# A buffer of its own for the second gate, the gates' results moved in memory, and two steps reordered in a hybrid attention and expert layer

## The chip, the cores and the metric

The kernel runs on one NeuronCore of one Trainium2 chip. The metric is the device time of one execution in microseconds (us). Five engines work side by side, each on its own list of instructions in order: TensorE (PE; its weight loads are listed as PEld), VectorE (DVE), ScalarE (ACT), GpSimd (POOL) and SyncE (SP), which here issues nearly all DMA transfers. They meet at semaphores only.

## What is computed

One encoder layer on 1024 tokens of width 1024, in float32. Cut to what matters here:

```python
# token mixing: branch A is gated linear attention, two directions per head, 4 heads
la_f = log_sigmoid(gaf @ gla_wa2_f + gla_ba_f) / 16      # first gate (forward)
la_b = log_sigmoid(gab @ gla_wa2_b + gla_ba_b) / 16      # second gate (backward)
o_a  = gla(q, k, v, la_f) + flip(gla(flip(q), flip(k), flip(v), flip(la_b)))
y_a  = (rmsnorm(o_a) * silu(gr)) @ w_gla_out
# branch B is a multi-head latent attention, y_b = o_b @ w_mla_out
g = sigmoid(gates)
x = x + (g[..., :D] * y_a + g[..., D:] * y_b) @ w_o      # the merge
# channel mixing: 16 experts, each takes the 128 tokens that suit it best
for e in range(16):
    rows = h[idx[e]]
    out[idx[e]] += vals[e] * ((silu(rows @ w_gate[e]) * (rows @ w_up[e])) @ w_down[e])
```

## The kernel before

Every large product is done as three matmuls (`three`, L825): each operand is split into a high part, rounded for TensorE's fast float32 mode, and a low part, what the rounding left. For weights ScalarE writes the high part (`dense_hi`, L1967; `split` of the experts, L2174) and VectorE subtracts it for the low part (`dense_lo`, L1381; `split`, L1800; both record their instruction at L1264). TensorE waits for the low part. The order of the work on each engine is written out by hand.

Three stretches matter.

**The heads of the gated attention** (`gla_head`, four of them: L992 on TensorE, L1537 on VectorE, L2031 on ScalarE). For each of two gates (d = 0, 1) TensorE makes the logits (L954), VectorE adds the bias into `zT` (`gate_bias`, L1541), ScalarE forms `eT` in three passes (L2053 to L2057), VectorE scans it into `bT` (L1563), subtracts half a chunk's value (L1570), and writes the tail, the distance to the end of the chunk, over `zT` (L1576). ScalarE then makes the exponentials `qt`, `kt` from `bT` and `kd` from `zT` (L2064 to L2067), copies the head's projected queries and keys (`take_qk`, L2034) and goes on to the second gate. VectorE's bias for d = 1 waits for that `kd` (`ed_ok`, L1544), because it overwrites `zT`. Meanwhile TensorE runs `project_vr` (L964): tiles 6 and 7 first, then 4 and 5, which need the banks of the second gate's logits and so wait for its bias (`z_dve`, L971), then 0 to 3, which wait for the copies of queries and keys (L973).

**The merge** (`job`, L1058): jobs in the order of `ORDER` (L59), four gates first, then outputs and gates in turn, 48 matmuls each. ScalarE takes a gate's logits through a sigmoid into `sg` (`gate`, L2098), two slots in turn. Gate job 2 writes the banks of gate 0, so it waits for that sigmoid (L1066). `sg` lies at the start of `merge_mem`, over `oaS`, the last head's output on its way to DRAM, so ScalarE waits at L2095 until this is stored (`oa_out`). The outputs come back as `mT` (L646, L650) and are split into `oT_hi` and `oT_lo` (`branch_hi` L2112, `branch_lo` L1679). SyncE stores the last head's output (L648), waits for it (L649), loads it again, and only then loads the weights of gate job 3 and on (L651).

**The start of the experts.** 24 units of 128 x 1024 weights per expert, in a ring of 8 slots for the split parts and 24 raw slots. VectorE splits units 0 to 15 (L1846), multiplies the first expert's gate and up products (`activate(0)`, L1848), and in `turn(0)` splits units 16 and on, with the low parts of the second expert's rows (`rows_in`, L1804) ahead of units 20 and 24. TensorE needs those halves before the units 16 and 20 (`gate`, L1208) and transposes `act_r` behind unit 20.

Of the kernel before, what the change touches and what calls it, by code (L numbers as in the profile page):

```python
# [8 lines left out]
P = 128  # L9
# [4 lines left out]
ALU = mybir.AluOpType  # L14
# [4 lines left out]
S = 1024  # L19
# [134 lines left out]
def hybrid_layer(nc, x, positions, g_mix, w_in, gla_wa2_f, gla_ba_f, gla_wa2_b, gla_ba_b, gla_onorm,  # L154
# [25 lines left out]
    with ExitStack() as ctx:  # L180
# [29 lines left out]
        with mix_mem:  # L210
# [69 lines left out]
            with late_mem:  # L280
# [10 lines left out]
                with gla_tmp:  # L291

                    out_mem = ExitStack()
                    with out_mem:
                        oaS = sb_in(out_mem, "oaS", [P, 2, S])
                    vr = sb_in(gla_tmp, "vr", [P, NT, 2 * DV])
                    qk_T = sb_in(gla_tmp, "qk_T", [P, 2, S])
                    qt = sb_in(gla_tmp, "qt", [P, 2, S])
                    kt = sb_in(gla_tmp, "kt", [P, 2, S])
                    kd = sb_in(gla_tmp, "kd", [P, 2, S])  # L300
                    zT = sb_in(gla_tmp, "zT", [P, S])
                    eT = sb_in(gla_tmp, "eT", [P, S])
                    bT = sb_in(gla_tmp, "bT", [P, S])
                    near = sb_in(gla_tmp, "near", [P, 2, NSC])
                    decay = sb_in(gla_tmp, "decay", [P, 2, NSC])
                    keep_hi = sb_in(gla_tmp, "keep_hi", [P, 2, P])
                    keep_lo = sb_in(gla_tmp, "keep_lo", [P, 2, P])
                    scan_m = sb_in(gla_tmp, "scan_m", [P, S])
                    kdR = qk_T[:, :, :].rearrange("p d (t c) -> p d t c", t=NT)
                    oR = kd[:, :, :].rearrange("p a (t c) -> p (a t) c", c=DV)  # L310
                    o_sqr = kt[:, :, :].rearrange("p a (t c) -> p (a t) c", c=DV)
                    att = bT[:, :].rearrange("p (t c) -> p t c", t=NT)
                    att_f = zT[:, :].rearrange("p (t c) -> p t c", t=NT)
                    att_b = eT[:, :].rearrange("p (t c) -> p t c", t=NT)
                merge_mem = ExitStack()
                with merge_mem:
                    sg = sb_in(merge_mem, "sg", [P, 2, S])
                    branch_mem = ExitStack()
# [938 lines left out]
        def _(dve):  # L1257
# [279 lines left out]
            def gla_head(h, first=False, more=True):  # L1537
# [3 lines left out]
                def gate_bias(d):  # L1541
                    dve.wait_ge(z_mm, h * 2 + d + 1)
                    if d == 1:
                        dve.wait_ge(ed_ok, h * 2 + 1)  # L1544
                    dve.tensor_scalar(zT[:].rearrange("p (a c) -> p a c", a=2), ps[:, 6 - 2 * d:8 - 2 * d, :],  # L1545
                                      b_a2[:, d:d + 1], None, ALU.add).then_inc(z_dve, 1)

                for d in range(2):
                    if d == 0:
                        gate_bias(0)  # L1550
                        if not first:
# [3 lines left out]
                    dve.wait_ge(z_act, h * 6 + 3 * d + 3)  # L1555
                    dve.scalar_tensor_tensor(out=eT[:], in0=zT[:], scalar=0.0, in1=eT[:], op0=ALU.min,
                                             op1=ALU.subtract).then_inc(ls_ok, 1)
# [16 lines left out]
                    if d == 1:  # L1574
                        dense_lo(4, mine)
                    dve.tensor_tensor(zT[:].rearrange("p (n c) -> p n c", c=P), last.broadcast_to((P, NSC, P)), b3,  # L1576
                                      ALU.subtract).then_inc(tail_ok, 1)
# [4 lines left out]
                    if d == 0:  # L1582
                        gate_bias(1)
                        dense_lo(3, mine)
                        dve.wait_ge(qk_ev, h * 4 + 4)
                    else:
                        dense_lo(5, mine)
# [238 lines left out]
            def turn(e, first=False, last=False):  # L1826
                for u in range(UNITS):
                    if first and u in (4, 8):
                        rows_in(1, (u // 4 - 1,))
                    split(FIRST + u, e)  # L1830
# [15 lines left out]
            for n in range(4, FIRST):  # L1846
                split(n)
            activate(0)  # L1848
            turn(0, first=True)
# [10 lines left out]
        def _(act):  # L1860
# [170 lines left out]
            def gla_head(h, first=False, last=False):  # L2031
# [17 lines left out]
                for d in range(2):  # L2049
                    act.wait_ge(z_dve, h * 2 + d + 1)  # L2050
                    if d == 1:
                        act.wait_ge(b_ok, h * 2 + 1)
                    nc.scalar.activation(eT[:], zT[:], ACT.Abs).then_inc(z_act, 1)  # L2053
                    act.wait_ge(z_act, h * 6 + 3 * d + 1)
# [11 lines left out]
                    act.wait_ge(tail_ok, h * 2 + d + 1)  # L2066
                    nc.scalar.activation(kd[:, d, :], zT[:], ACT.Exp, scale=1 / GATE_DIV).then_inc(ed_ok, 1)  # L2067
                    if d == 0:
# [25 lines left out]
            second_half_T(GH - 1, bank=4)  # L2094
            act.wait_ge(oa_out, 16 * GH)  # L2095

# [15 lines left out]
            def branch_hi(b, rows=range(KD)):  # L2112
                for k in rows:
                    if b:
                        act.wait_ge(stage_in[k % 2], 16 * (k // 2) + 16)
                    else:
                        act.wait_ge(oa_back, 16 if k < 6 else 32)
                    src = stage[:, k % 2, :] if b else mT[:, k, :]
                    nc.scalar.activation(oT_hi[:, k, :], src, ACT.Copy).then_inc(oT_hi_ok, 1)
# [86 lines left out]
            def turn(e, first=False, last=False):  # L2206
                for u in range(UNITS):
                    if first and u in (4, 8):
                        rows_in(1, (u // 4 - 1,))
                    split(FIRST + u, e)  # L2210
# [52 lines left out]
```

## Time and profile before

| | |
|---|---|
| time, median of 3 runs | 2054.45 us (2053.08 to 2058.4) |
| the profiled execution: its time, its span | 2054.51 us, 2052.8 us |
| mean granted TensorE clock | 0.981 of full |
| TensorE busy | 1939.7 us (94%) |
| VectorE busy | 1268.2 us (62%) |
| ScalarE busy | 981.9 us (48%) |
| GpSimd busy | 119.4 us (6%) |
| chain that ended last | TensorE 87%, VectorE 8%, ScalarE 2% |
| DMA, mean over the span | 148 GB/s, but 380 to 400 in the expert stretch |

The span runs from the first to the last instruction; the time has 1.7 us around it. Latent attention takes the time to about 590 us, the four heads to 970, the merge and the output projection to 1430, the choice of tokens to 1480, and the experts the rest. In the timeline's rows the columns are start, duration (both us), engine, line, operation, output<-input, shapes and count; in brackets stands the engine's idle time before it and what ended that.

### The profile page before, as it was taken

Reading aid. Unit: us, or ns where it says so; the run is one execution under the profiler, and the core shown is the slowest. Engines: PE = TensorE matmul, PEld = TensorE weight load, DVE = VectorE, ACT = ScalarE, POOL = GpSimd, SP = SyncE. Lnnn points to the kernel's source line nnn. Section 1 sums busy time; section 2 is a strip of 40 time slices with the busy share of each in tenths; the row PEclk is TensorE's granted clock in tenths of the full one; section 3 lists DMA queues with packets and bytes.
Section 4 is the critical chain, followed back from the end, with each engine's and each line's share of the span. In section 5 each row is a group of like instructions: output and inputs, shape, how many; then the busy total and the mean of one; then the engine's idle time right before and its main releaser. Section 6 shows DMA issues by size and latency. Waiting matters only on the chain.

```text
span 2052.8 us, 25988 instructions
## 1 busy us (share of the span) xinstructions
PE 1939.7 (94%) x9268; PEld 1605.5 (78%) x9268; DVE 1268.2 (62%) x1660; ACT 981.9 (48%) x1588; POOL 119.4 (6%) x127
## 2 busy tenths in 40 slices
PE   7989999999999999999899999999289999999997
PEld 5677888888778787878688888887278888888886
DVE  4157777777865646565311222432978989898986
ACT  4155555555454334242311211322268787878785
POOL 2010000000000000000000000000001010101010
PEclk9999999999999999999999999999699999999999
DMA  6000000000311111120412311152789999999992
GB/s 238 0 17 12 21 18 22 22 22 6 107 53 43 53 42 52 31 62 9 156 52 65 110 52 52 62 208 90 282 312 380 400 394 399 395 398 397 397 398 80
DMA packets 138658, 303.11 MB, mean 148 GB/s; under 512 B 16208, under 2 KB 70864, under 8 KB 138576
## 3 DMA queue, kind: packets, MB, share of 16 engines
q1 hardware_dynamic: 133968, 285.20, 37.3%
q0 software_dynamic: 4608, 16.78, 3.2%
q8 instruction: 55, 0.90, 0.2%
q14 instruction: 27, 0.22, 0.0%
HBM read 272.58 MB, written 29.36 MB: 147 GB/s over the span
## 4 chain that ended last, share of the span: by engine, by line
PE 87%; DVE 8%; ACT 2%; issue 1%; DMA 1%; POOL 1%; SPq 0%; DVEq 0%; ACTq 0%; POOLq 0%
PE ps L827 21%; PE ps L829 21%; PE ps L828 21%; PE ps L780 6%; PE ps L851 5%; PE ps L808 2%; PE ps L809 2%; PE ps L1042 1%; PE ps L885 1%; PE ps L884 1%; PE ps L1054 1%; DVE row_max L1445 1%; PE ps L1148 1%; PE ps L1026 1%; DVE top_i L1780 1%
## 5 line engine op out<-in xcount | busy, mean ns | idle before, releaser
L1264 DVE TENSOR_TENSOR w_lo<-w_raw,w_hi 128x1024 fp32r<-128x1024 f32 x384 | 442.7, 1218 | 57.8 <-ACT w_hi L2180 57.6
L2180 ACT ACTIVATE w_hi<-w_raw 128x1024 fp32r<-128x1024 f32 x384 | 370.9, 1052 | 12.6 <-PE ps L829 8.0
L1264 DVE TENSOR_TENSOR d_lo<-d_raw,d_hi 128x1024 fp32r<-128x1024 f32 x58 | 71.0, 1224 | 311.9 <-ACT d_hi L1972 311.8
L1972 ACT ACTIVATE d_hi<-d_raw 128x1024 fp32r<-128x1024 f32 x58 | 61.5, 1061 | 308.9 <-PE ps L829 296.9
L827 PE MATMUL ps<-w_hi,xeT_hi 128*128 128x512 f32 x512 | 201.8, 394 | 7.1 <-DVE xeT_lo L1264 7.1
L829 PE MATMUL ps<-w_hi,xeT_lo 128*128 128x512 f32 x512 | 200.1, 391 | 0.0
L828 PE MATMUL ps<-w_lo,xeT_hi 128*128 128x512 f32 x512 | 200.0, 391 | 0.0
L827 PE MATMUL ps<-hT_parts,d_hi 128*128 128x512 f32 x384 | 152.2, 396 | 8.5 <-ACT sg L2105 7.7
L828 PE MATMUL ps<-hT_parts,d_hi 128*128 128x512 f32 x384 | 150.6, 392 | 0.0
L829 PE MATMUL ps<-hT_parts,d_lo 128*128 128x512 f32 x384 | 150.6, 392 | 0.0
L1445 DVE TENSOR_REDUCE row_max<-ps 128x1 f32<-128x1024 f32 x64 | 78.3, 1224 | 106.6 <-PE ps L885 105.9
L723 POOL TENSOR_TENSOR stat<-stat,minus_half 128x1 f32<-128x1 f32 (+3 forms) x48 | 57.2, 1191 | 1286.0 <-DVE stat L1261 1286.0
L827 PE MATMUL ps<-d_hi,hT_parts 128*128 128x512 f32 x288 | 113.8, 395 | 6.9 <-DVE zT L1545 6.9
L827 PEld LDWEIGHTS ps<-w_hi,xeT_hi 128*128 128x128 f32 x512 | 96.7, 189 | 27.1 <-issue 6.3
L828 PE MATMUL ps<-d_lo,hT_parts 128*128 128x512 f32 x288 | 112.8, 392 | 0.0
L829 PE MATMUL ps<-d_hi,hT_parts 128*128 128x512 f32 x288 | 112.7, 391 | 0.0
L829 PEld LDWEIGHTS ps<-w_hi,xeT_lo 128*128 128x128 f32 x512 | 96.5, 189 | 20.3
L828 PEld LDWEIGHTS ps<-w_lo,xeT_hi 128*128 128x128 f32 x512 | 96.7, 189 | 19.5
L827 PE MATMUL ps<-w_hi,act_T_hi 128*128 128x512 f32 x256 | 101.0, 395 | 0.8 <-ACT ye L2203 0.8
L828 PE MATMUL ps<-w_lo,act_T_hi 128*128 128x512 f32 x256 | 99.7, 389 | 0.0
L829 PE MATMUL ps<-w_hi,act_T_lo 128*128 128x512 f32 x256 | 99.7, 389 | 0.0
L827 PE MATMUL ps<-oT_hi,d_hi 128*128 128x512 f32 x256 | 99.6, 389 | 0.0
(313 smaller groups left out, 4006.7 us busy)
## 6 DMA issues: line engine op xcount, KB each, us to landing
w_raw<-in_w_gate_e SPq DMA_DIRECT2D x128, 512.0 KB, 8.0
w_raw<-in_w_up_e SPq DMA_DIRECT2D x128, 512.0 KB, 7.5
w_raw<-in_w_down_e SPq DMA_DIRECT2D x128, 512.0 KB, 6.7
d_raw<-in_w_in SPq DMA_DIRECT2D x80, 256.0 KB, 3.0
xs<-in_x SPq DMA_DIRECT2D x8, 512.0 KB, 6.9
rows_T<-hT SPq DMA_DIRECT2D x1, 4096.0 KB, 12.8
mla_out_T<-obS SPq DMA_DIRECT2D x16, 256.0 KB, 2.0
carry<-rows_T SPq DMA_DIRECT2D x1, 4096.0 KB, 14.2
```

The source lines that it names most:

```text
L723: pool.tensor_tensor(dst, dst, minus_half[:, 0:dst.shape[1]], ALU.pow).then_inc(done, 1)
L780: ins = pe.transpose(ps[0:rows, bank, j * P:(j + 1) * P], src, ident[:])
L808: pe.matmul(ps[:, a, 0:LA], lhs, w_lat[:, k, 0:LA], start=k == 0, stop=k == KD - 1)
L809: mm = pe.matmul(ps[:, b, 0:LB], lhs, w_lat[:, k, LA:LAT], start=k == 0, stop=k == KD - 1)
L827: pe.matmul(out_ap, a_hi, b_hi, start=start, stop=False)
L828: pe.matmul(out_ap, a_hi, b_lo, start=False, stop=False)
L829: return pe.matmul(out_ap, a_lo, b_hi, start=False, stop=stop)
L851: mm = pe.matmul(ps[:, bank, j * width:(j + 1) * width], src[:, k, t * P:(t + 1) * P], w[:, k, :], start=k == 0, stop=k == kc - 1)
L1264: return dve.tensor_tensor(dst, whole, high.bitcast(F32), ALU.subtract)
L1445: dve.tensor_reduce(row_max[:, n:n + 1], ps[:, 2 * (n % 2):2 * (n % 2) + 2, :], mybir.AxisListType.XY, ALU.max, negate=True).then_inc(max_ ...
L1972: nc.scalar.activation(d_hi[:, n % 2, :], d_raw[:, n % 2, :], ACT.Copy).then_inc(d_hi_ok, 1)
L2180: nc.scalar.activation(w_hi[:, n % RING, :], w_raw[:, n % RAW, :], ACT.Copy).then_inc(hi_ok, 1)
```

## The change

Four edits, none of which adds or removes arithmetic.

- The second gate's biased logits go to a buffer of their own, `zT_back`; the wait for `ed_ok` is gone, and VectorE adds that bias ahead of the first gate's tail instead of behind the decay.
- `sg` moves behind the place of `oT_hi` and `oT_lo` (16 x S + HALF elements further on), and so no longer lies over `oaS`. ScalarE's wait for the store stands now in front of the copies into `oT_hi`, behind the first two gates' sigmoids.
- VectorE takes the low parts of the second expert's rows ahead of units 16 and 18 instead of 20 and 24, and `activate(0)` ahead of unit 19 instead of ahead of 16.
- ScalarE takes the second half of those rows ahead of unit 22 instead of 24.

```diff
--- before.py
+++ after.py
@@ -299,6 +299,7 @@
                     kt = sb_in(gla_tmp, "kt", [P, 2, S])
                     kd = sb_in(gla_tmp, "kd", [P, 2, S])
                     zT = sb_in(gla_tmp, "zT", [P, S])
+                    zT_back = sb_in(gla_tmp, "zT_back", [P, S])
                     eT = sb_in(gla_tmp, "eT", [P, S])
                     bT = sb_in(gla_tmp, "bT", [P, S])
                     near = sb_in(gla_tmp, "near", [P, 2, NSC])
@@ -314,7 +315,10 @@
                     att_b = eT[:, :].rearrange("p (t c) -> p t c", t=NT)
                 merge_mem = ExitStack()
                 with merge_mem:
-                    sg = sb_in(merge_mem, "sg", [P, 2, S])
+                    sg_mem = ExitStack()
+                    with sg_mem:
+                        sb_in(sg_mem, "below_sg", [P, 16 * S + HALF])
+                        sg = sb_in(sg_mem, "sg", [P, 2, S])
                     branch_mem = ExitStack()
                     with branch_mem:
                         oT_hi = sb_in(branch_mem, "oT_hi", [P, KD, S], F32R)
@@ -1540,9 +1544,7 @@
 
                 def gate_bias(d):
                     dve.wait_ge(z_mm, h * 2 + d + 1)
-                    if d == 1:
-                        dve.wait_ge(ed_ok, h * 2 + 1)
-                    dve.tensor_scalar(zT[:].rearrange("p (a c) -> p a c", a=2), ps[:, 6 - 2 * d:8 - 2 * d, :],
+                    dve.tensor_scalar((zT, zT_back)[d][:].rearrange("p (a c) -> p a c", a=2), ps[:, 6 - 2 * d:8 - 2 * d, :],
                                       b_a2[:, d:d + 1], None, ALU.add).then_inc(z_dve, 1)
 
                 for d in range(2):
@@ -1553,7 +1555,8 @@
                         dense_lo(2, mine)
 
                     dve.wait_ge(z_act, h * 6 + 3 * d + 3)
-                    dve.scalar_tensor_tensor(out=eT[:], in0=zT[:], scalar=0.0, in1=eT[:], op0=ALU.min,
+                    z = (zT, zT_back)[d]
+                    dve.scalar_tensor_tensor(out=eT[:], in0=z[:], scalar=0.0, in1=eT[:], op0=ALU.min,
                                              op1=ALU.subtract).then_inc(ls_ok, 1)
                     dve.wait_ge(ls_ok, h * 2 + d + 1)
 
@@ -1573,14 +1576,15 @@
                     last = b3[:, :, 0:1] if d else b3[:, :, P - 1:P]
                     if d == 1:
                         dense_lo(4, mine)
-                    dve.tensor_tensor(zT[:].rearrange("p (n c) -> p n c", c=P), last.broadcast_to((P, NSC, P)), b3,
+                    else:
+                        gate_bias(1)
+                    dve.tensor_tensor(z[:].rearrange("p (n c) -> p n c", c=P), last.broadcast_to((P, NSC, P)), b3,
                                       ALU.subtract).then_inc(tail_ok, 1)
                     dve.wait_ge(e_ok, h * 6 + 3 * d + 2)
                     e3 = qt[:, d, :].rearrange("p (n c) -> p n c", c=P)
                     s.link(dve.tensor_tensor(decay[:, d, :].unsqueeze(2), e3[:, :, 0:1] if d else e3[:, :, P - 1:P],
                                              near[:, d, :].unsqueeze(2), ALU.mult))
                     if d == 0:
-                        gate_bias(1)
                         dense_lo(3, mine)
                         dve.wait_ge(qk_ev, h * 4 + 4)
                     else:
@@ -1825,8 +1829,10 @@
 
             def turn(e, first=False, last=False):
                 for u in range(UNITS):
-                    if first and u in (4, 8):
-                        rows_in(1, (u // 4 - 1,))
+                    if first and u in (0, 2):
+                        rows_in(1, (u // 2,))
+                    if first and u == 3:
+                        activate(0)
                     split(FIRST + u, e)
                     if u == (8 if first else 2) + LEAD - 1:
                         act_in(e, 0)
@@ -1845,7 +1851,6 @@
             rows_in(0)
             for n in range(4, FIRST):
                 split(n)
-            activate(0)
             turn(0, first=True)
             with dve.Fori(1, NE - 2) as e:
                 turn(e)
@@ -2050,7 +2055,7 @@
                     act.wait_ge(z_dve, h * 2 + d + 1)
                     if d == 1:
                         act.wait_ge(b_ok, h * 2 + 1)
-                    nc.scalar.activation(eT[:], zT[:], ACT.Abs).then_inc(z_act, 1)
+                    nc.scalar.activation(eT[:], (zT, zT_back)[d][:], ACT.Abs).then_inc(z_act, 1)
                     act.wait_ge(z_act, h * 6 + 3 * d + 1)
                     nc.scalar.activation(eT[:], eT[:], ACT.Exp, scale=-1.0).then_inc(z_act, 1)
                     act.wait_ge(z_act, h * 6 + 3 * d + 2)
@@ -2064,7 +2069,7 @@
                     nc.scalar.activation(qt[:, d, :], bT[:], ACT.Exp, scale=1 / GATE_DIV).then_inc(e_ok, 1)
                     nc.scalar.activation(kt[:, d, :], bT[:], ACT.Exp, scale=-1 / GATE_DIV).then_inc(e_ok, 1)
                     act.wait_ge(tail_ok, h * 2 + d + 1)
-                    nc.scalar.activation(kd[:, d, :], zT[:], ACT.Exp, scale=1 / GATE_DIV).then_inc(ed_ok, 1)
+                    nc.scalar.activation(kd[:, d, :], (zT, zT_back)[d][:], ACT.Exp, scale=1 / GATE_DIV).then_inc(ed_ok, 1)
                     if d == 0:
                         take_qk()
                         dense_hi(3, mine)
@@ -2092,7 +2097,6 @@
                 gla_head(h)
             gla_head(GH - 1, last=True)
             second_half_T(GH - 1, bank=4)
-            act.wait_ge(oa_out, 16 * GH)
 
 
             def gate(b, i):
@@ -2114,6 +2118,7 @@
                     if b:
                         act.wait_ge(stage_in[k % 2], 16 * (k // 2) + 16)
                     else:
+                        act.wait_ge(oa_out, 16 * GH)
                         act.wait_ge(oa_back, 16 if k < 6 else 32)
                     src = stage[:, k % 2, :] if b else mT[:, k, :]
                     nc.scalar.activation(oT_hi[:, k, :], src, ACT.Copy).then_inc(oT_hi_ok, 1)
@@ -2205,8 +2210,8 @@
 
             def turn(e, first=False, last=False):
                 for u in range(UNITS):
-                    if first and u in (4, 8):
-                        rows_in(1, (u // 4 - 1,))
+                    if first and u in (4, 6):
+                        rows_in(1, (u // 2 - 2,))
                     split(FIRST + u, e)
                     if u == LEAD - 1 and not first:
                         results(e - 1)
```

## Rows read from the trace of the kernel before

**Rows 1.** TensorE's waits: who waited for whom, us in total, times, longest.

```profile
PE ps L827 <- ACT sg L2105: 7.7, 1, 7.7
PE ps L827 <- DVE xeT_lo L1264: 7.1, 2, 6.1
PE ps L827 <- DVE zT L1545: 6.9, 4, 2.1
```

**Rows 2.** Timeline of TensorE, merge, matmuls at full clock.

```profile
1014.53 0.39 PE L828 MATMUL ps<-hT_parts,d_hi 128*128 128x512 f32 x1
...
1015.66 0.39 PE L827 MATMUL ps<-oT_hi,d_hi 128*128 128x512 f32 x1
```

**Rows 3.** Timelines of VectorE, ScalarE and TensorE, second head.

```profile
703.06 1.23 DVE L1576 TENSOR_TENSOR zT<-bT 128x1024 f32<-128x1024 f32 x1
...
706.22 1.28 DVE L1545 TENSOR_SCALAR zT<-ps,b_a 128x1024 f32<-128x1024 f32 x1 [1.79 <-ACT kd L2067]
...
706.02 2.04 ACT L2038 ACTIVATE qk_T<-ps 128x512 f32<-128x512 f32 x4
...
707.56 0.50 PE L827 MATMUL ps<-d_hi,hT_parts 128*128 128x512 f32 x1 [2.01 <-DVE zT L1545]
```

**Rows 4.** Timeline of TensorE, third and fourth head, at tile 4.

```profile
800.81 0.50 PE L827 MATMUL ps<-d_hi,hT_parts 128*128 128x512 f32 x1 [1.98 <-DVE zT L1545]
...
893.83 0.50 PE L827 MATMUL ps<-d_hi,hT_parts 128*128 128x512 f32 x1 [2.08 <-DVE zT L1545]
```

**Rows 5.** Busy time by stretch, fourth head: length, engines (instructions), PEclk, DMA share, GB/s.

```profile
894.00:898.00 4.00, 4.00 (x11) 3.15 (x12) 2.72 (x3) 3.94 (x5) 0.00 (x0) 0.57 0.12 16
```

**Rows 6.** Timelines of TensorE, ScalarE and VectorE, start of the merge.

```profile
982.96 0.39 PE L829 MATMUL ps<-hT_parts,d_lo 128*128 128x512 f32 x1
...
987.49 1.06 ACT L1972 ACTIVATE d_hi<-d_raw 128x1024 fp32r<-128x1024 f32 x1 [8.73 <-DMA gla_out_T<-oaS]
...
989.86 1.02 ACT L2105 ACTIVATE sg<-ps 128x1024 f32<-128x1024 f32 x1
994.14 1.06 ACT L1972 ACTIVATE d_hi<-d_raw 128x1024 fp32r<-128x1024 f32 x1 [3.26 <-DMA d_raw<-in_w_in]
...
995.23 1.23 DVE L1264 TENSOR_TENSOR d_lo<-d_raw,d_hi 128x1024 fp32r<-128x1024 f32 x1 [5.42 <-ACT d_hi L1972]
997.10 9.18 DVE L1264 TENSOR_TENSOR oT_lo<-carry,oT_hi 128x1024 fp32r<-128x1024 f32 x8 [0.64 <-ACT oT_hi L2119]
```

**Rows 7.** Chain of work that ended last, start of the merge: start, us, what.

```profile
973.15 5.62 DMA d_raw<-in_w_in
```

**Rows 8.** Timelines of VectorE, ScalarE and TensorE, start of the experts.

```profile
1495.48 5.76 DVE L1264 TENSOR_TENSOR w_lo<-w_raw,w_hi 128x1024 fp32r<-128x1024 f32 x5 [4.50 <-ACT w_hi L2180]
1504.91 1.23 DVE L1814 TENSOR_TENSOR act_r<-ps,silu_g 128x1024 f32<-128x1024 f32 x1 [3.67 <-PE ps L829]
...
1510.60 0.68 DVE L1264 TENSOR_TENSOR xeT_lo<-ps,xeT_hi 128x512 fp32r<-128x512 f32 x1
...
1502.93 0.58 ACT L2187 ACTIVATE xeT_hi<-ps 128x512 fp32r<-128x512 f32 x1
1503.41 3.89 ACT L2180 ACTIVATE w_hi<-w_raw 128x1024 fp32r<-128x1024 f32 x4
...
1511.38 0.77 PE L827 MATMUL ps<-w_hi,xeT_hi 128*128 128x512 f32 x1 [6.13 <-DVE xeT_lo L1264]
...
1525.36 0.39 PE L827 MATMUL ps<-w_hi,xeT_hi 128*128 128x512 f32 x1
```

**Rows 9.** Busy time by stretch, a stretch of expert turns; columns as in rows 5.

```profile
1606.00:1639.00 33.00, 33.00 (x152) 27.43 (x151) 29.59 (x30) 26.78 (x30) 3.62 (x2) 1.00 1.03 396
```

**Rows 10.** The raw weights' tile: duration ns min/median/max, first and last start us.

```profile
L2180 ACT ACTIVATE w_hi<-w_raw x384: 1039/1052/1065, 1437.5 to 2035.1; 128x1024 fp32r<-128x1024 f32 x192
...
L687 SPq DMA_DIRECT2D w_raw<-in_w_down_e x128: 327/333/333, 1488.9 to 2004.9; - x128
```

**Rows 11.** DMA issues of the page: count, KB each, us to landing.

```profile
w_raw<-in_w_gate_e SPq DMA_DIRECT2D x128, 512.0 KB, 8.0
```

## The prediction

> **What bounds the kernel now.** TensorE does. The table of the page gives it 94% of the span and lets nearly the whole chain of work that ended last run over it, so a change can win only where TensorE stands still. I therefore read the list of TensorE's waits first. It is led by waits that the diff does not touch (the top-k search, the start); below them stand the three of [rows 1], 7.7, 7.1 and 6.9 us in total. Each belongs to a place that the diff edits. Then I read, engine by engine, the timeline around the three. Two numbers serve throughout. A matmul of 512 columns starts every 0.226 us at full clock (five slots between 1014.53 and 1015.66 [rows 2]). A record of such a matmul lasts 0.39 us, so a wait shown as idle costs 0.39 - 0.23 = 0.16 us more in starts than the idle says.
>
> **Part A, the second gate's buffer.** In each head of the gated attention, TensorE does tiles 6 and 7 of the value product and then waits at tile 4 for the bias of the second gate's logits (L971). That bias step (L1545) writes zT, which ScalarE still reads for kd of the first gate, so VectorE waits for kd. In the second head VectorE idles 1.79 us, starts the bias at 706.22, and TensorE goes on at 707.56 after 2.01 us idle [rows 3]. With zT_back the step needs only z_mm and VectorE's own place, now right behind the subtraction of L1570, that is where the tail (L1576) begins today: 703.06. It takes 1.28 us and ends at 704.34, while TensorE is ready at 705.55. The wait goes entirely: 2.17 us of starts in this head, 2.14 and 2.24 in the third and fourth (1.98 and 2.08 idle [rows 4]). The list has 6.9 us for four waits [rows 1], so the first is 6.9 - 2.01 - 1.98 - 2.08 = 0.83, or 0.99 in starts. Sum 7.5 us. A first matmul after a wait takes 0.34 us of its slot instead of 0.23 (0.1 us, three heads: 0.3). In the fourth head the granted clock is 0.57 in the four microseconds behind the wait, level 1.2 GHz for most of it: 11 matmuls start in 4.00 us where 17.6 fit [rows 5], a loss of 6.6 x 0.23 = 1.5 us, with the edges 1.8. **A = 9.6 us.** I take that clock loss as caused by the wait, since nothing else stands still there; its bounds are 0 and 1.8. The Trainium skill, "TensorE: Matmul & The Clock Gate", section "What's actually happening", says that how many matmuls run slowly is run-variable. By that rule the third head's wait without a slow stretch and the fourth's with one would be chance, and A could be 7.8 as well as 9.6; the trace (one of three equal waits) agrees.
>
> What A delays: the tail moves 1.14 us back on VectorE (the bias's 1.28 less the overlap of neighbouring records) and ends at 704.20 + 1.23 = 705.43. ScalarE's kd, which today runs in the 0.95 us before 706.02, waits for it and comes 0.4 us later, and so does all that is queued behind it: the four copies of qk_T (2.04 us, first done now near 706.9), d_hi of the next unit, the second gate's Abs. TensorE wants the first copy at tile 0, twelve matmuls behind tile 4: 705.4 + 2.7 = 708.1, so there is 1.2 us to spare. VectorE's own idle time in front of d_lo L1264 takes up the bias step. Price zero; if that cover were gone it would cost at most the 0.4 us a head, 1.6.
>
> **Part B, the merge.** ScalarE waits at L2095 until the last head's output is stored, because sg lies over oaS. It stands 8.73 us until 987.49, then does d_hi, the table load and sg, ready at 989.86 + 1.02 = 990.88 [rows 6]. TensorE, out of work at 982.96 + 0.23 = 983.19, needs both d_lo and that sg for gate job 2. With sg elsewhere the wait moves to branch_hi, behind the first two gates. ScalarE is free at 978.76; the unit it needs landed at 978.77 (973.15 + 5.62 [rows 7]). The same block then runs 8.7 us earlier: sg at 982.15, d_lo near 981.1. Job 2 starts at 983.19 with no wait, and takes 48 x 0.226 = 10.9 us to 994.1.
> What is late next: gate job 3. The diff leaves SyncE's order alone, and there job 3's load is still queued behind the wait for the store (over at 987.49). Its d_hi starts at 994.14, when the load lands, its d_lo ends at 995.23 + 1.23 = 996.46 [rows 6]. So job 3 starts at 996.55, after a new wait of 2.5 us, and ends at 1007.4. Output job 0 needs oT_lo (997.10 + 9.18 = 1006.28) and the d_lo that follows it, done at 1007.4: just in time. The load for it is issued a microsecond sooner, behind job 3's, which may cost that one 0 to 0.5 us. Output job 0 starts today at 1015.66 and then at 1007.5: 8.2 us. The new 2.5 us wait is the size of those in [rows 4], one of which was followed by a slow stretch and one not, so I take half of 1.8 off: **B = 7.3 us**, bounds 8.2 and 6.0.
> ScalarE's moved wait has the eight oT_hi copies behind it, as before; by then (996) the store is long done, so it costs nothing.
>
> **Part C, the first experts.** VectorE has the lows of units 0 to 15 done at 1495.48 + 5.76 = 1501.24, then stands 3.67 us for activate(0), does four lows, and at 1510.60 the first half of the rows (0.68 us), with four more lows ahead of the second. TensorE waits 6.13 us for the first half and restarts at 1511.38 [rows 8]. In the new order the first half follows xeT_hi at 1503.51 and ends at 1504.2. A low takes 5.76 / 5 = 1.15 us (1.23 the last), so 16 and 17 end at 1505.4 and 1506.5. TensorE, free at 1505.25, starts near 1505.45. ScalarE now gives the second xeT_hi after two splits (1503.41 + 2 x 0.95 = 1505.3, done near 1505.95), VectorE the second low at 1507.1, low 18 at 1508.25, activate(0) at 1508.2 to 1509.4, low 19 at 1510.55. A unit takes TensorE 6 x 0.227 = 1.36 us, so it wants low 19 at 1509.7 and waits 0.9 us there, a small new wait; the transposes of act_r behind unit 20 find it ready. Counting on (three units to 1512.0 incl. that wait, a fourth, 0.8 us of transposes, three more), the next product starts at 1518.35 instead of 1525.36. **C = 7.0 us**, bounds 6 (clock low after 0.9 us) and 8 (no wait at 19). The loads of units 40 and on are issued about 2 us sooner, as lows 16 and on are.
>
> **Sum** against the profiled execution's own 2054.51 us (span 2052.8 and 1.7 around it; the median is 2054.45, so no correction): 9.6 + 7.3 + 7.0 = 23.9, and 2054.5 - 23.9 = 2030.6.
>
> **The rivals.**
> 1. A larger new wait in the merge. Job 3's load is a chain of store, 1 MB load and unit load that nothing shortens. If it lands 0.5 us later and TensorE runs all of its first stretch at the low level, B is 5; if A's clock loss also turns up elsewhere, 4.1 us are missing: 2034.7. For it: the DMA wait of 3.26 us at this very place [rows 6]. Against: its landing is set by transfers that the diff does not move.
> 2. C is hidden by transfers. In the expert turns the DMA queues are full: share 1.03, 396 GB/s, while TensorE is also busy 33.00 of 33 us [rows 9]. If the loads bound the turns, starting 7 us earlier would be given back: 2054.5 - 16.9 = 2037.6. Against: the last load is issued at 2004.9 and the last split starts at 2035.1 [rows 10], 30 us, of which a landing takes 8.0 [rows 11].
> 3. Slower than before. The same loads slow down once two expert turns are pushed together. A turn moves 24 units, a gather and a scatter of 0.524 MB each, 13.6 MB, in 13.6 / 0.396 = 34.4 us. 22 us of lead over 14 turns stand against this rival, so a turn of loads may grow from 34.4 to 36.0 us before TensorE feels it; from 37.7 us on it has eaten the 23.9 us too. A rate lower by a tenth makes the turn 38.2: 14 x 3.8 = 53, less 22 and 24, gives +7, or 2061. Nothing in the rows makes the rate fall so far.
> The Trainium skill, "DMA: Bandwidth & Descriptors", section "Where 436 GB/s comes from", holds that transfers from HBM are bound near 358 GB/s a core, which would be a turn of about 38 us and this rival's time. The trace disagrees, with 396 GB/s over whole turns.
> 4. The change does not do what it says: in A the bias still comes late, since it sits behind the scan. Then 2040; the 1.2 us between 704.34 and 705.55 speaks against.
>
> **How the numbers follow.** Forecast 0.76 (2028 to 2033), rival 1 0.11, rival 2 0.06, rival 3 0.02, rival 4 0.02, anything else 0.03. The low end takes all upper bounds (9.6 + 8.2 + 8 = 25.8: 2028.7) less a microsecond for the spread of runs; the high end reaches rival 2. About 0.3% (6 us) is what a measurement of this kernel tells from no change. Only cases that lose 18 us of the 24 come within it.
>
> **What would show it.** Right: no wait for zT at L827 in four heads; bias before tail on VectorE; no sg wait, but one near 994 of 2 to 3 us for d_lo, ended by a load; the wait for xeT_lo below 0.5 us and one near 1 us for w_lo; expert turns still of 34.4 us. Wrong: a wait for qk_T at tile 0, a split waiting for w_raw in later turns, slow stretches in new places.

## The result, and the profile after

| | before | after |
|---|---|---|
| time, median | 2054.33 us (2053.08 to 2058.4, 4 runs) | 2033.99 us (2033.06 to 2035.2, 4 runs) |
| the profiled execution: its time, its span | 2054.51 us, 2052.8 us | 2035.2 us, 2033.5 us |
| TensorE busy | 1939.7 us (94%) | 1934.6 us (95%) |

The ratio is 0.9898, 95% interval 0.9881 to 0.9915. The time lies 3.4 us above the forecast of 2030.6. That is 1.0 us above the 2028 to 2033 that the prediction gave for its forecast case, and inside its whole range, whose high end reaches the 2037.6 of rival 2. Between the two profiled executions lie 19.3 us, where 23.9 were forecast.

I cut the span at five instants of TensorE, read from its timeline, in every kernel alike: the first matmul of the first head's gate logits (L954); the start of the second half of gate job 1, 24 matmuls before the wait of [rows 1]; the first matmul of an output job (`oT_hi`); the first of the experts; and the first of the second expert's up product, the one at 1525.36 in [rows 8].

| stretch, us | before | after | won | forecast |
|---|---|---|---|---|
| start to the heads | 598.27 | 598.89 | -0.6 | 0 |
| heads (part A) | 379.38 | 369.24 | 10.1 | 9.6 |
| start of the merge (part B) | 38.01 | 35.21 | 2.8 | 7.3 |
| merge, output projection, choice of tokens | 466.60 | 466.31 | 0.3 | 0 |
| first expert (part C) | 43.10 | 36.19 | 6.9 | 7.0 |
| from there to the end | 527.44 | 527.66 | -0.2 | 0 |

So the whole shortfall lies in B. The list of TensorE's waits of the kernel after (who waited for whom, us in total, times, longest):

```profile
PE ps L784 <- DVE xs L1273: 13.5, 1, 13.5
PE ps L831 <- ACT sg L2109: 5.4, 1, 5.4
...
PE ps L831 <- DVE xeT_lo L1268: 1.0, 1, 1.0
PE ps L831 <- DVE w_lo L1268: 0.9, 2, 0.6
```

Against [rows 1]: the wait for zT is gone from it, xeT_lo fell from 7.1 to 1.0 us, and sg fell from 7.7 only to 5.4, where the prediction had it at zero. The wait for xs is the kernel's opening load; it differs from run to run, and with it the -0.6 of the first row.

Part A, the second head, VectorE's timeline of after:

```profile
701.75 0.69 DVE L1573 TENSOR_TENSOR bT<-bT,near 128x512 f32<-128x512 f32 x1
702.57 1.28 DVE L1547 TENSOR_SCALAR zT_back<-ps,b_a 128x1024 f32<-128x1024 f32 x1
703.77 1.22 DVE L1581 TENSOR_TENSOR zT<-bT 128x1024 f32<-128x1024 f32 x1
```

The bias stands directly behind the subtraction, where the tail stood in [rows 3], with no idle time in brackets. ScalarE's `kd` of this gate now waits 0.44 us for the tail, where the prediction had 0.4, and nothing behind it is late. From the first gate logits on, TensorE has no idle time over 0.15 us in the four heads and no slow stretch (a row of matmuls that start 0.43 us apart instead of 0.23, at the 1.2 GHz level).

Part B, the start of the merge, ScalarE, then TensorE, of after:

```profile
967.98 1.27 ACT L2033 ACTIVATE oaS<-ps,onorm_c 128x512 f32<-128x512 f32 x2 [4.82 <-PE ps L784]
975.66 1.06 ACT L1977 ACTIVATE d_hi<-d_raw 128x1024 fp32r<-128x1024 f32 x1 [6.42 <-DMA d_raw<-in_w_in]
976.74 1.28 ACT L2109 ACT_TABLE_LOAD   x1
978.03 1.02 ACT L2109 ACTIVATE sg<-ps 128x1024 f32<-128x1024 f32 x1
...
973.44 0.39 PE L833 MATMUL ps<-hT_parts,d_lo 128*128 128x512 f32 x1
979.20 0.77 PE L831 MATMUL ps<-hT_parts,d_hi 128*128 128x512 f32 x1 [5.37 <-ACT sg L2109]
979.76 0.63 PE L832 MATMUL ps<-hT_parts,d_hi 128*128 128x512 f32 x1
```

ScalarE is free at 969.2 and no longer waits for the store `gla_out_T<-oaS`, as in [rows 6], but for a load: the weights of gate job 2. That load lands at 975.6, and the same block of d_hi, table load and sg follows it unshortened. TensorE then stands 5.37 us and starts at the lower clock level: the stretch 979 to 984 (length, engines with their instructions, granted clock, DMA share, GB/s) has 11 matmuls and a granted clock of 0.50, the 1.2 GHz level.

```profile
979.00:984.00 5.00, 4.80 (x11) 3.80 (x12) 0.00 (x0) 0.05 (x1) 0.00 (x0) 0.50 0.92 308
```

Where the load comes from is in the view of SyncE's own issues (start, time for issuing, line) and in the view of DMAs for 945 to 975 us of after (count, size, median us from issue to landing):

```profile
962.62 0.37 SPq L650 DMA_DIRECT2D carry<-gla_out_T  x1
963.03 1.09 SPq L541 DMA_DIRECT2D d_raw<-in_w_in  x2
969.32 0.39 SPq L613 DMA_DIRECT2D gla_out_T<-oaS  x1
```

```profile
carry<-gla_out_T SPq DMA_DIRECT2D x1, 3072.0 KB, 11.5
gla_out_T<-oaS SPq DMA_DIRECT2D x1, 1024.0 KB, 8.8
d_raw<-in_w_in SPq DMA_DIRECT2D x2, 256.0 KB, 11.5
```

Half a megabyte of weights takes 11.5 us, as long as the 3 MB return issued 0.4 us before it. The same view of before, 955 to 985 us, has it too, and the prediction did not use it:

```profile
carry<-gla_out_T SPq DMA_DIRECT2D x1, 3072.0 KB, 11.4
gla_out_T<-oaS SPq DMA_DIRECT2D x1, 1024.0 KB, 8.6
d_raw<-in_w_in SPq DMA_DIRECT2D x2, 256.0 KB, 11.6
```

Issued at 972.56 and 973.1, the load of before landed near 985.0, only 2.5 us ahead of the store at 987.49. That is what moving sg could win while the load stays where it is. TensorE's wait fell by 7.7 - 5.4 = 2.3 us. Behind it 11 matmuls started at the low level where before there were 13, which is another 0.4 us of the 2.8.

Part C, the start of the experts, VectorE and TensorE of after:

```profile
1490.96 0.69 DVE L1268 TENSOR_TENSOR xeT_lo<-ps,xeT_hi 128x512 fp32r<-128x512 f32 x1 [2.29 <-ACT xeT_hi L2192]
...
1493.84 0.68 DVE L1268 TENSOR_TENSOR xeT_lo<-ps,xeT_hi 128x512 fp32r<-128x512 f32 x1
...
1495.57 1.22 DVE L1818 TENSOR_TENSOR act_r<-ps,silu_g 128x1024 f32<-128x1024 f32 x1
...
1492.93 0.47 PE L831 MATMUL ps<-w_hi,xeT_hi 128*128 128x512 f32 x1 [0.26 <-DVE w_lo L1268]
...
1497.98 0.50 PE L831 MATMUL ps<-w_hi,xeT_hi 128*128 128x512 f32 x1 [0.61 <-DVE w_lo L1268]
```

The 6.13 us of [rows 8] have become 0.26 and 0.61, and the next product starts 6.9 us sooner. About 2 of the 6.9 us are a slow stretch: in before, the first ten matmuls behind the 6.13 us wait take 4.4 us (1511.38 to 1515.78) instead of 2.3, and after has no such stretch here. Two of them, TensorE of before, 0.43 us apart:

```profile
1511.94 0.63 PE L828 MATMUL ps<-w_lo,xeT_hi 128*128 128x512 f32 x1
1512.37 0.63 PE L829 MATMUL ps<-w_hi,xeT_lo 128*128 128x512 f32 x1
```

A stretch of the expert turns, columns as in [rows 9]:

```profile
1594.00:1627.00 33.00, 33.00 (x155) 27.50 (x154) 29.58 (x30) 25.61 (x29) 3.61 (x2) 1.00 1.03 396
```

The turns run as before: TensorE full, 396 GB/s.

### The profile page after: what moved, and what is told of

It is laid out like the page before. It is cut to its first block, busy times and chain, and to the rows that moved or that the text cites. A ratio compares the mean times of both kernels' runs of the same rounds, so it can differ in the third digit from the quotient of the medians.

```text
span 2033.5 us, 25996 instructions
## 1 busy us (share of the span) xinstructions
PE 1934.6 (95%) x9268; PEld 1602.6 (79%) x9268; DVE 1267.1 (62%) x1660; ACT 981.8 (48%) x1588; POOL 120.1 (6%) x127
## 3 DMA queue, kind: packets, MB, share of 16 engines
q1 hardware_dynamic: 133968, 285.20, 37.5%
## 4 chain that ended last, share of the span: by engine, by line
PE 89%; DVE 6%; ACT 2%; DMA 1%; issue 1%; POOL 1%; SPq 0%; DVEq 0%; ACTq 0%; POOLq 0%
PE ps L831 22%; PE ps L833 22%; PE ps L832 22%; PE ps L784 6%; PE ps L855 5%; PE ps L812 2%; PE ps L813 2%; PE ps L1046 1%; PE ps L889 1%; PE ps L888 1%; PE ps L1058 1%; DVE row_max L1449 1%; PE ps L1152 1%; PE ps L1030 1%; DMA d_raw<-in_w_in 1%
## 5 line engine op out<-in xcount | busy, mean ns | idle before, releaser
L832 PEld LDWEIGHTS ps<-w_lo,xeT_hi 128*128 128x128 f32 x512 | 96.2, 188 | 19.3
```

The source lines that it names most:

```text
L832: pe.matmul(out_ap, a_hi, b_lo, start=False, stop=False)
```

## The experiments

Every result below is a median; the kernel before, run beside them on the same chips, had medians of 2054.65 to 2054.93 us; in brackets stand the ratio to it and its 95% interval. The kernel after was not run again beside them, so differences to it are best read from the stretches. These are the ones of the table above, each from one profiled execution. The theory they start from: A, B and C are independent, and B is short because the load of gate job 2 lands with the 3 MB ahead of it. The rivals: the parts disturb one another; B is short because of the store, of ScalarE's block, or of the 1 MB behind it.

**One part at a time.** The first kernel is before plus part A whole, the second leaves out the bias step's new place:

```diff
+                    zT_back = sb_in(gla_tmp, "zT_back", [P, S])
...
-                    if d == 1:
-                        dve.wait_ge(ed_ok, h * 2 + 1)
...
+                    else:
+                        gate_bias(1)
```

> Part A alone, on the kernel before. The two traces put it at 10.1 us (the last matmul ahead of the merge's wait starts at 973.44 instead of 982.96, and the run's heads began 0.6 us later), where the prediction had 9.6. Theory: the parts act at separate places and add up, so 2054.3 - 10.1 = 2044.2, and no slow stretch of TensorE in the fourth head. Rival: the fourth head's slow stretch was chance; then it turns up again somewhere in the heads and the gain is near 8 us, 2046.

> The second gate's buffer without the move: the bias stays behind the decay on VectorE. Theory: what held the bias back was the wait for kd, not its place; without it, it starts at once behind the decay, about 1.4 us later than in the full change, and ends some 0.2 us after TensorE is ready in heads two to four. Gain 8.5 to 9.5 us, 2045.3; TensorE waits for zT 0.2 us in three heads and not in the first. Rival: the place is what counts and the buffer alone gives less than half, above 2049.

Measured: 2043.72 us (0.9937, 0.9921 to 0.9954) and 2045.67 (0.9956, 0.9939 to 0.9973). The heads took 369.23 us with the whole of A, as in the kernel after, and 370.79 with the buffer alone. So the buffer carries 8.6 of the 10.1 us (1.6 of them the slow stretch in the fourth head), the new place of the bias 1.5. TensorE's waits of the second kernel show what is left without it:

```profile
PE ps L828 <- DVE zT_back L1544: 1.0, 3, 0.3
```

Three waits of 0.3 us; the first head has none. Neither kernel has a slow stretch in the heads.

The third kernel is before with `sg` moved and the wait in its new place (the diff's `sg_mem` and `oa_out` lines), the fourth is before with the new orders of the experts alone (the diff's two `turn` hunks):

> Part B alone. The traces put it at 2.8 us (from the last matmul ahead of the wait to output job 0: 32.7 before, 29.9 after), not 7.3. Theory: the same here, 2051.5, because the load of gate job 2 lands about 12 us after its issue and its d_hi, the table load and sg come only then; TensorE's wait is 5.4 us, and ScalarE waits for a load ahead of that d_hi. Rival: B is worth 7 us by itself and lost in the changed kernel because the heads end earlier; then 2047.

> Part C alone. The traces put it at 6.9 us from the first expert matmul to the second expert's up product (43.1 before, 36.2 after). Theory: 2054.3 - 6.9 = 2047.4, expert turns as before, and the wait for xeT_lo gone. Rival: the loads give part of it back over the turns once nothing else is changed; then 2049 or more and a later stretch of TensorE waiting for low parts.

Measured: 2052.33 us (0.9986, 0.9976 to 0.9995) and 2048.68 (0.9971, 0.996 to 0.9983). The start of the merge took 34.90 us, 3.1 less than before, the first expert 36.12, 7.0 less. Both kernels keep the heads of before, and there lost 1.6 us more than before did (380.94 and 380.98): two of the three 2.0 us waits for zT were followed by a slow stretch instead of one. ScalarE and TensorE in the third kernel:

```profile
987.49 1.06 ACT L1975 ACTIVATE d_hi<-d_raw 128x1024 fp32r<-128x1024 f32 x1 [6.39 <-DMA d_raw<-in_w_in]
...
991.02 0.77 PE L830 MATMUL ps<-hT_parts,d_hi 128*128 128x512 f32 x1 [5.33 <-ACT sg L2107]
```

The same wait for the same load, without A and C. The parts add up: 10.15 + 3.11 + 6.98 = 20.2 against 19.9 for the three together over the same stretches. The rival of parts that disturb one another falls.

**The load alone.** The kernel after with the load of gate job 2 ahead of the wait for the heads' stores and so ahead of the 3 MB, then with those of jobs 2 and 3:

```diff
-            load_jobs(0, 0, 2)
+            load_jobs(0, 0, 4)
             sp.wait_ge(oa_out, 16 * (GH - 1))
...
-            load_jobs(0, 2, 3)
             store_oa(GH - 1)
...
-            load_jobs(0, 3, JOBS)
+            load_jobs(0, 4, JOBS)
```

(shown for both jobs; for job 2 alone the bounds are 3, and the last call stays.)

> The changed kernel with one more edit: SyncE issues the load of gate job 2 ahead of the 3 MB return of the first six output tiles instead of behind it. Theory: that load was late because it shares the DMA queues with the 3 MB ahead of it. It has then long landed, ScalarE does d_hi, table load and sg right behind its copies of oaS, and TensorE's wait of 5.4 us in front of gate job 2 is gone, with the slow stretch behind it. Next late is gate job 3, with a wait of about 2.5 us. B becomes what was predicted for it: output job 0 starts 5.4 us sooner, 2034.0 - 5.4 = 2028.6. Rival: the load was not the cause (the table load and the sigmoid behind the copies of oaS are); then the wait stays and the time is 2034.

> As the run before, and the load of gate job 3 too ahead of the 3 MB return, so ahead of SyncE's wait for the store. Theory: both waits of TensorE in front of gate jobs 2 and 3 are gone, the copies into oT_hi start near 976 and wait only for the last 1 MB of the return near 983, the lows and the unit of output job 0 are ready before gate job 3 ends, so output job 0 starts about 7.8 us sooner than in the changed kernel: 2026.2. Rival: the later return of the outputs, now behind 1 MB of loads, becomes the bound, and this run is no better than the one before, 2028.6.

Measured: 2027.76 us (0.9864, 0.9848 to 0.9881), start of the merge 28.67 us; and 2027.11 (0.986, 0.9843 to 0.9876), 27.29 us. The kernel with job 2 alone, ScalarE and TensorE:

```profile
966.84 1.06 ACT L1976 ACTIVATE d_hi<-d_raw 128x1024 fp32r<-128x1024 f32 x1
967.92 1.28 ACT L2108 ACT_TABLE_LOAD   x1
...
981.11 1.06 ACT L1976 ACTIVATE d_hi<-d_raw 128x1024 fp32r<-128x1024 f32 x1 [10.87 <-DMA d_raw<-in_w_in]
...
983.48 0.50 PE L830 MATMUL ps<-hT_parts,d_hi 128*128 128x512 f32 x1 [1.06 <-DVE d_lo L1267]
```

ScalarE takes job 2's unit with no idle time, and TensorE's first wait is now the one for job 3, 1.06 us. It was expected at 2.5; the store that job 3's load waits for takes 7.6 us here instead of 8.8 in the kernel after. With both loads early it is gone too: 120 matmuls from the second half of gate job 1 to the first output job take 120 x 0.227 = 27.2 us, and 27.29 were measured. These two kernels differ from the one after by the place of loads only, and win 6.5 and 7.9 us in that stretch. The landing was the cause; the table load and the sigmoid, the rival, run as before and cost TensorE nothing.

**The load alone, without the new place of sg.** Before with both loads early (the same edit):

> The kernel before with only the reordered loads of gate jobs 2 and 3. Theory: there ScalarE stands for the store until 987.5 in any case, so gate job 2 starts as late as before; nothing is gained, 2054.3 within 1 us, and the two obstacles only pay together. Rival: the loads alone held the merge up, and the sg move was not needed; then 2046 to 2049.

Measured: 2053.08 us (0.9992, 0.9982 to 1.0002), start of the merge 35.98 us, 2.0 less than before. ScalarE and the DMA view, 950 to 985 us:

```profile
984.86 1.06 ACT L1971 ACTIVATE d_hi<-d_raw 128x1024 fp32r<-128x1024 f32 x1 [7.59 <-DMA gla_out_T<-oaS]
```

```profile
gla_out_T<-oaS SPq DMA_DIRECT2D x1, 1024.0 KB, 7.5
```

I had expected no change in that stretch. The store still decides, as expected, but it lands after 7.5 us instead of 8.6 once the half megabyte is not in the queues, and TensorE's wait for sg falls from 7.69 to 6.54 us. That is 1.1 of the 2.0 us. The other 0.8 are a shorter slow stretch behind the wait (9 matmuls instead of 13), and its length differs from run to run. ScalarE's wait for job 3's load [rows 6] is gone too, but TensorE never stood for it. In the whole time the 2.0 us cannot be told from nothing. So both steps are needed: sg's new place alone gives 2.8 to 3.1 us, the early loads alone 1.1 to 2.0, together 10.7 (38.01 to 27.29).

**How much is ahead of it.** The kernel after with the 3 MB return cut into 1 and 2 MB and job 2's load between them:

```diff
+            sp.dma_start(mT[:, 0:2, :], oa_dram[0:2].rearrange("k p s -> p k s")).then_inc(oa_back, 16)
             load_jobs(0, 2, 3)
+            sp.dma_start(mT[:, 2:6, :], oa_dram[2:6].rearrange("k p s -> p k s")).then_inc(oa_back, 16)
...
-                        act.wait_ge(oa_back, 16 if k < 6 else 32)
+                        act.wait_ge(oa_back, 48)
```

(With three returns instead of two, ScalarE now awaits all of them before its first copy into `oT_hi`. In its list that copy stands behind the units of gate jobs 2 and 3, so it does not touch the waits read here.)

> The changed kernel with the 3 MB return cut in two: 1 MB, then the load of gate job 2, then 2 MB. It doses the suspected cause. Theory: the load's landing follows the bytes ahead of it: 12.0 us behind 3 MB, about 6 us behind 1 MB, which is just when ScalarE is free, so TensorE's wait of 5.4 us is nearly or wholly gone and the time near 2029. Rival: landing does not depend on what is ahead (the load is slow for its own row pattern); then the wait stays at 5 us and the time at 2034.

Measured: 2031.12 us (0.9876, 0.9859 to 0.9892), start of the merge 31.19 us. DMA view (940 to 975 us) and TensorE:

```profile
carry<-gla_out_T SPq DMA_DIRECT2D x1, 1024.0 KB, 5.0
d_raw<-in_w_in SPq DMA_DIRECT2D x2, 256.0 KB, 5.5
```

```profile
986.66 0.50 PE L832 MATMUL ps<-hT_parts,d_hi 128*128 128x512 f32 x1 [1.97 <-DVE d_lo L1269]
...
988.28 0.63 PE L832 MATMUL ps<-hT_parts,d_hi 128*128 128x512 f32 x1
```

Behind 1 MB the load lands in 5.5 us, behind 3 MB in 11.5, behind nothing large (the kernel with both loads early) in 3.0: its landing follows what was issued before it. The 2 MB issued right behind it did not hold it up. What the store, issued 6 us behind the load in the kernel after, adds to its 11.5 us, no run separates. The Trainium skill, "DMA: Bandwidth & Descriptors", section "Two DMAs through the same engine are not ordered", says that within one queue of one DMA engine descriptors start in order, though an earlier one may still be writing when a later one completes; the three landings agree with the starts. This kernel is also the picture that the prediction drew: job 2 without a wait, then a wait of 1.97 us for job 3 with a slow stretch of eight matmuls. The expected 2029 us left that second wait out. Its B is 38.01 - 31.19 = 6.8 us, inside the predicted 6.0 to 8.2. Its first expert took 37.74 us, 1.5 more than after, with a slow stretch of eight matmuls at its first product.

**The first expert.** Three kernels. First, after with both early loads and `activate(0)` at `u == 5`; second, before with VectorE's part of the new order but not ScalarE's; third, after with `activate(0)` left where it was:

```diff
-                    if first and u == 3:
+                    if first and u == 5:
                         activate(0)
```

```diff
-                    if first and u in (4, 8):
-                        rows_in(1, (u // 4 - 1,))
+                    if first and u in (0, 2):
+                        rows_in(1, (u // 2,))
+                    if first and u == 3:
+                        activate(0)
```

```diff
-                    if first and u == 3:
-                        activate(0)
...
+            activate(0)
             turn(0, first=True)
```

> The changed kernel with both loads of gate jobs 2 and 3 ahead of the last store (2027.1 us, of which first expert product to second expert's up product 36.1 us), and activate(0) two units later on VectorE, ahead of unit 21 instead of 19. Theory: the small new waits of TensorE for low 17 and low 19 (0.26 and 0.61 us) are what is left of part C; with activate(0) behind low 20 the second is gone and the transposes of act_r, behind unit 20, still find it done or wait at most 0.5 us: the stretch takes 35.5 us, the time is about 2026.5. Rival: activate(0) is the later one now, the transposes wait for it, about 1.2 us; the stretch takes 36.5 to 37 us, the time is 2027.5 to 2028.

> The kernel before with VectorE's half of part C alone: low parts of the rows ahead of units 16 and 18, activate(0) ahead of 19. ScalarE takes the second half of the rows ahead of unit 24 as before, that is two splits (about 1.9 us) later than in the changed kernel. Theory: VectorE waits for that half at unit 18 and everything behind it comes 1.3 to 2 us later, TensorE waits for it at unit 20: the stretch takes 37.5 to 38 us instead of 36.1 (changed) and 43.1 (before); the time is about 2049 to 2049.5. Rival: ScalarE's move is not needed, its second half is early enough: 36.1 us.

> The changed kernel but with activate(0) ahead of unit 16, as before; the low parts of the rows stay ahead of 16 and 18. Theory: most of part C comes from taking activate(0) away from the head of VectorE's list, where it waits 3.67 us for TensorE's product: with it there, low 16 comes about 2.5 to 3 us later, TensorE waits 2.5 to 3.5 us at the start of the second expert, and the stretch takes 38.5 to 39.5 us (40.5 with a slow stretch behind the wait) instead of 36.2; the time is about 2036.5 to 2038. Rival: the gain lies in the places of the low parts of the rows alone (with eight low parts fewer ahead of them), and the stretch stays within 0.5 us of 36.2.

Measured: 2026.45 us (0.9868, 0.9851 to 0.9884), 2049.33 (0.9976, 0.9966 to 0.9985), 2037.17 (0.9923, 0.9906 to 0.994). The stretch took 35.18, 37.52 and 39.29 us, all as the theory had them or a little better: 35.5, 37.5 to 38, and 38.5 to 39.5. (The wait of 0.26 us that the first expectation puts at low 17 is at low 16.) In the third kernel a slow stretch of eight matmuls (1.6 us) is part of the 39.29, which I had priced on top. VectorE and TensorE of the third kernel:

```profile
1490.09 1.22 DVE L1818 TENSOR_TENSOR act_r<-ps,silu_g 128x1024 f32<-128x1024 f32 x1 [3.67 <-PE ps L833]
...
1493.19 0.47 PE L831 MATMUL ps<-w_hi,xeT_hi 128*128 128x512 f32 x1 [2.77 <-DVE w_lo L1268]
```

VectorE stands in front of `activate(0)` the same 3.67 us as in [rows 8], everything it owes comes later, and TensorE waits 2.77 us. So of C's 6.9 us, 43.10 - 39.29 = 3.8 come from the earlier low parts of the rows and 3.1 from moving `activate(0)` away, 1.6 of them that slow stretch. ScalarE's edit is worth 37.52 - 36.19 = 1.3 us of them: without it VectorE stands 1.31 us for the second half and TensorE 1.18. With `activate(0)` two units later still, the 0.61 us wait goes and the transposes find act_r ready. The gain in the stretch is 0.9 us (36.12 with both loads early, 35.18 here); the medians of 2026.45 and 2027.11 do not by themselves tell it from nothing. This kernel has the lowest median of all and is 7.5 us faster than the changed one.

## Why the prediction was right or wrong

**The bound.** Right. TensorE is 95% busy, and the idle time that went, with the slow stretches behind it, came off the span: the rows outside the three parts moved by 0.6 us at most.

**Part A, 10.1 us against 9.6.** Right, step by step. From head to head, logits to logits, before and after differ by 1.2, 2.3 and 2.3 us for the first three, where the sum had 1.0, 2.3 and 2.2. The fourth head gave 4.3, where the sum had 4.1: its wait and the slow stretch behind it. I had taken that stretch as caused by the wait, with zero as its other bound, and the runs bear this out. Five kernels have the waits (before, and those with sg's place, the experts' order, VectorE's half of it or the early loads alone): 7 of their 15 waits of 2.0 us were followed by a slow stretch. In the eight kernels without such waits there is none in the heads' value products. Which wait is followed changes from run to run, so A would have come out near 8.5 or 11.7 us against a profiled execution of before with no such stretch or with two; that it had just the one is luck. The Trainium skill, "TensorE: Matmul & The Clock Gate", section "What's actually happening", calls the number of slow matmuls at a kernel's start run-variable; here the same holds behind a short wait. A second stretch in the heads cost 380.95 - 379.4 = 1.6 us. The delay of the tail cost nothing, as said: no wait for qk_T is in the list.

**Part B, 2.8 us against 7.3. This step failed:** "the unit it needs landed at 978.77 (973.15 + 5.62 [rows 7])", and with it "Job 2 starts at 983.19 with no wait". The 5.62 us is a piece of the chain of waits, and such a piece ends where the chain goes over to something else. Here it goes over at 978.83, the instant at which the last store was issued; the next piece of the chain is that store. The chain thus said nothing of when the load landed. It landed near 985.0, and the DMA view gives it (11.6 us). With that number the prediction's own steps give: d_hi at 985.0 instead of 987.49, sg 2.5 us sooner, TensorE's wait 7.7 - 2.5 = 5.2 (measured: 5.4). The slow stretch behind the wait stays. With B = 2.5 the sum is 19.1 and the forecast 2035.4; the profiled execution took 2035.2, the median is 2033.99. Of the prediction's signs of being right two did not come: sg's wait stayed, and no wait for d_lo near 994 appeared.

The rest of B was right, which the experiment with 1 MB ahead shows: once the load is there, job 2 starts at once, and the wait for job 3 is 1.97 us with a slow stretch (2.5 and half a chance of one were forecast). In the kernel after it did not appear, because job 2 itself started 5.5 us later and covered it. Rival 1 placed a larger wait at job 3; its time of 2034.7 is near the result, but by another mechanism and at another place, and it is not borne out. What happened to B belongs under "anything else", which had a chance of 0.03. The range held the time because A and C were right within half a microsecond and B was short by only 4.5 us, not because this case had been seen.

**Part C, 6.9 us against 7.0.** Right. TensorE waits 0.26 us for low 16, where 0.2 was forecast (1505.25 to 1505.45), and 0.61 for low 19 instead of 0.9. The 1.0 of xeT_lo in the list is the first expert's own, of the 7.1 of [rows 1] less 6.1. No slow stretch followed the two small waits, as in the forecast and not as in its lower bound of 6.

**The other rivals.** Rival 2 (C hidden by transfers) and rival 3 (loads slower) would show in the last stretch: 527.44 before, 527.66 after, 527.4 to 527.7 in every kernel run. Nothing is given back, and the turns run at 396 GB/s, where the Trainium skill's "DMA: Bandwidth & Descriptors", section "Where 436 GB/s comes from", has HBM bind near 358; here the measurement decides. Rival 4 (the bias still late): no gap at tile 4.

**What stays open.** The start to the heads took 595.4 to 601.2 us over the profiled executions, without any edit there; that is most of the few microseconds by which runs of one kernel differ. Its cause was not looked into.

## What to carry to other kernels

A piece of the chain of waits tells how long the chain rested on a transfer, not when that transfer landed; take landings from the DMA view, and for each load that is about to become the last thing awaited, look at what the same queue was given just before it. When a buffer is moved so that one wait goes, move the small loads ahead of the large ones in the same step: here each alone gave 1 to 3 us and both together 10.7. In an engine's ordered list, put the step that must wait for another engine behind the steps that others already wait for: that alone was 3.1 us in the first expert, half of it a slow stretch.

## What the runs showed of the hardware

- A load of half a megabyte issued 0.4 us behind 3 MB lands with it: in 11.5 to 11.8 us in eight kernels, against 5.5 behind 1 MB and 3.0 to 3.2 behind nothing large. A 1 MB store issued 6 us behind that load took 8.6 to 9.2 us in these eight, and 7.5 to 7.8 in the four with the half megabyte away. In the kernel with 1 MB ahead of the load it took 8.5.
- Idle time of 2.0 us in the heads was followed, in 7 of 15 cases, by seven to nine matmuls of 512 columns at the 1.2 GHz level (0.43 us from start to start), about 1.6 us lost; the waits of 0.3 and 0.6 us never were. The wait of 0.97 us before the first expert product, 9 us behind one of 35.8 us, was followed by eight in one of 13 kernels. The wait of 5.37 us was followed by eleven, the first of them included.
